# Hybrid decoder step: the output projection's weights in single blocks, a tenth expert weight buffer, token rows stored before their scaling

## What is computed

```python
# cut from the reference
proj = rmsnorm(x, norm_mix) @ w_in                # z, x/B/C, dt, u
y_ssd, y_s5 = SSD_group(proj), S5_group(proj)     # 1024 columns each, each with its own rmsnorm
x = x + concatenate([y_ssd, y_s5], -1) @ w_out    # w_out is 2048 x 1024
t = rmsnorm(x, norm_ffn)
g = argmax(t @ rc_w + rc_b)                       # one of 4 groups of experts
pick the best 2 of the group's 8 experts; gates = p_group * normalised softmax
for e in range(32):                               # w_gate, w_up 1024 x 512; w_down 512 x 1024
    out += gates[:, e:e+1] * ((silu(t @ w_gate[e]) * (t @ w_up[e])) @ w_down[e])
y = rmsnorm(x + out, norm_final)
```

## Time and profile before

| | us |
|---|---|
| median of 3 runs | 1072.44 |
| lowest and highest run | 1067.82, 1073.02 |
| the profiled execution, its own time | 1061.96 |
| its span, first to last instruction | 1059.7 |

### The profile page before, as it was taken

One profiled execution on the slowest core, in us unless ns is written; L12 is line 12 of the kernel. 1 busy time (PEld: TensorE's weight loads), 2 busy tenths in 40 slices (PEclk: granted clock), 3 DMA queues, 4 the chain that ended last, 5 costly groups with the idle time before them and its releaser, 6 DMA issues.

```text
span 1059.7 us, 17219 instructions
## 1 busy us (share of the span) xinstructions
PE 961.3 (91%) x6496; PEld 682.0 (64%) x6497; DVE 434.8 (41%) x743; ACT 331.1 (31%) x662; POOL 268.0 (25%) x510
## 2 busy tenths in 40 slices
PE   6999999999999999999999999999877788998881
PEld 5889779877776788998765555555443444554440
DVE  6999877454466898951521111111100101111112
ACT  3025323453325784322422222232212121222113
POOL 1000888888421010000012222222222112222110
PEclk9999999999999999999999999999999999999996
DMA  7585172110098744255589999999999999999994
GB/s 268 125 142 92 29 121 81 41 63 22 12 223 226 254 147 175 87 238 239 218 323 392 396 383 398 385 394 397 395 396 395 396 413 404 409 410 408 425 385 167
DMA packets 73566, 277.54 MB, mean 262 GB/s; under 512 B 36953, under 2 KB 38873, under 8 KB 56497
## 3 DMA queue, kind: packets, MB, share of 16 engines
q1 hardware_dynamic: 63020, 252.67, 65.0%
q0 software_dynamic: 8720, 19.86, 6.8%
q10 hardware_dynamic: 1780, 4.41, 1.1%
HBM read 260.17 MB, written 25.61 MB: 270 GB/s over the span
## 4 chain that ended last, share of the span: by engine, by line
PE 68%; DMA 23%; DVE 5%; issue 2%; ACT 1%; POOL 0%; SPq 0%; ACTq 0%; POOLq 0%; DVEq 0%
PE ps L653 24%; DMA sb_arena<-w_up 20%; PE ps L1023 9%; PE ps L1037 7%; PE ps L1016 7%; PE ps L919 7%; PE ps L992 2%; DMA sb_arena<-ssm_in 2%; PE ps L685 1%; PE ps L741 1%; PE ps L798 1%; DVE sb_arena L1960 1%; PE ps L772 1%; PE ps L895 1%; PE ps L1030 1%
## 5 line engine op out<-in xcount | busy, mean ns | idle before, releaser
L653 PE MATMUL ps<-sb_arena 128*128 128x264 f32 (+1 forms) x1152 | 266.9, 392 | 9.1 <-DMA sb_arena<-wi 9.1
L653 PEld LDWEIGHTS ps<-sb_arena 128*128 128x128 f32 x1152 | 218.8, 191 | 57.5 <-DMA sb_arena<-wi 9.6
L1956 DVE TENSOR_TENSOR sb_s5b<-sb_s5b,ps 128x256 f32<-128x256 f32 x36 | 22.2, 617 | 408.0 <-PE ps L1023 408.0
L1023 PE MATMUL ps<-sb_arena 128*64 128x256 f32 x1152 | 131.3, 380 | 22.0 <-DMA sb_arena<-w_up 22.0
L1037 PE MATMUL ps<-sb_arena 128*64 128x512 f32 x576 | 131.5, 598 | 20.7 <-DVE sb_arena L1960 20.7
L1016 PE MATMUL ps<-sb_arena 128*64 128x256 f32 x1152 | 132.6, 383 | 16.5 <-DMA sb_arena<-w_gate 15.8
L1016 PEld LDWEIGHTS ps<-sb_arena 128*64 128x64 f32 x1152 | 83.6, 138 | 76.3 <-DMA sb_arena<-w_gate 27.0
L1023 PEld LDWEIGHTS ps<-sb_arena 128*64 128x64 f32 x1152 | 82.5, 137 | 67.1 <-DMA sb_arena<-w_up 28.9
L1388 ACT ACTIVATE sb_kxf<-ps,sb_gate_of 64x512 f32<-64x512 f32 x36 | 24.6, 683 | 301.1 <-PE ps L1037 301.1
L1037 PEld LDWEIGHTS ps<-sb_arena 128*64 128x64 f32 x576 | 39.0, 136 | 90.1 <-issue 60.9
L1415 DVE TENSOR_TENSOR sb_arena<-sb_arena 128x64 f32<-128x64 f32 (+12 forms) x86 | 78.0, 907 | 19.5 <-DMA sb_arena<-ssm_in 12.2
...
...
## 6 DMA issues: line engine op xcount, KB each, us to landing
sb_arena<-w_gate SPq DMA_DIRECT2D x32, 2048.0 KB, 33.7
sb_arena<-w_up SPq DMA_DIRECT2D x32, 2048.0 KB, 35.9
sb_arena<-w_down SPq DMA_DIRECT2D x32, 2048.0 KB, 35.6
sb_arena<-wi SPq DMA_DIRECT2D x28, 512.0 KB, 4.0
sb_arena<-w_out SPq DMA_DIRECT2D x4, 2048.0 KB, 8.5
sb_arena<-ssm_in POOLq DMA_DIRECT2D x8, 512.0 KB, 8.9
sb_arena<-wglu SPq DMA_DIRECT2D x8, 512.0 KB, 5.0
o_ssm_s<-sb_arena POOLq DMA_DIRECT2D x8, 512.0 KB, 4.0
```

The lines of the kernel that those rows point to most:

```text
L653: last = mm(ps[:, b0 + h, 0:t1 - t0], ring[w % 3][:, k, :], src[:, k, t0:t1], start=k == 0, stop=k == KD - 1)
L1023: last = mm(ps[64 * r:64 * r + 64, 1, 0:256], xt[:, k, :], Wu[s][:, k, 256 * r:256 * r + 256], start=k == 0, stop=k == KD - 1)
L1956: V.tensor_tensor(hh.rearrange("p (j c) -> p c j", j=2), sg.rearrange("p (c j) -> p c j", j=2), ps[:, 1, 0:256].rearrange("p (c j) -> p c ...
```

## The change

`w_out` comes in sixteen loads of 512 KB, one for each block (8 x 128 columns per partition, so rows of 512 bytes), into three raw buffers; the low part of each block lies in place in them, and there are two high parts, one of them in the array kxf. A block's load waits until block o-3 is done, its high part on ACT until block o-2 is done, and PE waits before each block for its low part. The high and low parts are put one by one into the lists of ACT and DVE.

The space that this frees holds a tenth expert buffer, `Wg_first`, for the gate weights of expert 0; the three slots `Wg` then hold the gates of experts 1, 2, 3 and so on. SP's list is reordered: up 1 is loaded at the start of the projection, gate 0 when the S5 gate products are done, then up 0, gate 1, down 0 and gate 3 between the blocks' loads, down 1 when block 15 is done, then the stores into sum_scr, which no longer wait for x_scr, and then gate 2, up 2 and down 2. The refills go up, down and then the next expert's gate.

The rows are stored into x_scr as they are. ACT's five scalings are gone; the one-hot table of the first tile is multiplied with the root (oh0), and a third table, oh_root, made by DVE and ten more matmuls, gives each slot's root, which ACT applies when it copies a gathered tile. The gathered rows now lie where the rows x1 were, so POOL's first gathers wait for the stores into sum_scr as well, and the first tile's copies wait until both tables are finished (oh_done 2).

```diff
-        wo = [part(14944, KD, 512), part(4096, KD, 512)]
-        wo_hi, wo_lo, y_hi, y_lo = (
+        wo = [part(14944 + 1024 * i, KD, P) for i in range(3)]
+        wo_lo, y_hi, y_lo = (
             [rounded(f"{name}{i}", off, KD, w) for i, off in enumerate(offs)] for name, w, offs in (
-                ("wo_hi", 512, (39920, 26736)), ("wo_lo", 512, (14944, 4096)),
+                ("wo_lo", P, (14944, 15968, 16992)),
                 ("y_hi", N, (35632, 22448)), ("y_lo", N, (10656, 30832))))
...
+        Wg_first = part(4096, KD, FF)
+        xg = [part(1024 * i, D, p=(0, T)) for i in range(RING)]
         xst = part(8384, D, p=(0, T))
         xt = part(9408, KD, T)
         ht = part(9920, 2, P)
-        Lt = part(4288, N, p=(0, 36))
-        xs = [part(o, D) for o in (4824, 5848, 6872, 19040, 20064)]
-        first = part(21088, D, p=(0, T))
+        Lt = part(9806, N, p=(0, 36))
+        first = xst
+        root_of = part(10176, IDXC, p=(0, T))
...
+        kxf_at = -(-nc.sbuf_base // 32) * 32
         kxf = sb("kxf", [P, 2048 + 1024])
+        wo_hi = [rounded("wo_hi0", 18016, KD, P),
+                 nc.alloc_sbuf_tensor_at("sb_wo_hi1", [P, KD, P], F32R, offset=kxf_at)]
...
-            def wo_load(q):
-                sp.dma_start(wo[q % 2], wsrc[:, 8 * (q // 2):8 * (q // 2) + 8,
-                                             512 * (q % 2):512 * (q % 2) + 512]).then_inc(wo_ld[q % 2], 16)
+            def wo_load(o):
+                sp.dma_start(wo[o % 3], wsrc[:, 8 * (o // 8):8 * (o // 8) + 8,
+                                             P * (o % 8):P * (o % 8) + P]).then_inc(wo_ld[o % 3], 16)
             sp.wait_ge(gelu_done, 8)
-            wo_load(0)
+            for o in range(3):
+                wo_load(o)
...
+            sp.wait_ge(hn_done, NS)
+            sp.dma_start(Wu[1], usrc[1]).then_inc(wu_ld[1], 16)
+
+            def next_wo(o):
+
+                sp.wait_ge(o_mm, o - 2)
+                wo_load(o)
+
+            next_wo(3)
             sp.wait_ge(y2_done, 8)
-            sp.wait_ge(wide_done, NW)
-            wo_load(1)
-            sp.wait_ge(o_mm, 4)
-            wo_load(2)
+            sp.dma_start(Wg_first, gsrc[0]).then_inc(ld_x[0], 16)
+            for o in range(4, 7):
+                next_wo(o)
             sp.wait_ge(ms_done, 3)
             sp.dma_start(gf, a["gffn"].rearrange("(k p) -> p k", p=P), allow_slow_non_contiguous=True).then_inc(moe_ld, 16)
             sp.dma_start(g8, a["gffn"].rearrange("(p k) -> p k", k=KD)).then_inc(moe_ld, 16)
             sp.dma_start(wr, a["wr"].rearrange("p (k n) -> p k n", k=KD)).then_inc(moe_ld, 16)
             sp.dma_start(brow, a["br"].rearrange("c o -> (c o)").partition_broadcast(P)).then_inc(moe_ld, 16)
-            sp.wait_ge(o_mm, 8)
-            wo_load(3)
-            sp.dma_start(Wg[0], gsrc[0]).then_inc(wg_ld[0], 16)
-            sp.dma_start(Wg[2], gsrc[2]).then_inc(wg_ld[2], 16)
-            sp.wait_ge(o_mm, 12)
+            for o in range(7, 11):
+                next_wo(o)
             sp.dma_start(Wu[0], usrc[0]).then_inc(wu_ld[0], 16)
+            next_wo(11)
+            next_wo(12)
+            sp.dma_start(Wg[0], gsrc[1]).then_inc(wg_ld[0], 16)
+            next_wo(13)
+            next_wo(14)
             sp.dma_start(Wd_to[0], dsrc[0]).then_inc(wd_ld[0], 16)
-            sp.dma_start(Wu[2], usrc[2]).then_inc(wu_ld[2], 16)
+            next_wo(15)
+            sp.dma_start(Wg[2], gsrc[3]).then_inc(wg_ld[2], 16)
             sp.wait_ge(o_mm, 16)
-            sp.dma_start(Wg[1], gsrc[1]).then_inc(wg_ld[1], 16)
-            sp.dma_start(Wu[1], usrc[1]).then_inc(wu_ld[1], 16)
             sp.dma_start(Wd_to[1], dsrc[1]).then_inc(wd_ld[1], 16)
-            sp.wait_ge(xs_st, 80)
+            sp.wait_ge(x1t_ev, 10)
             for i, (t0, n) in enumerate(TT):
                 sp.dma_start(sum_scr[t0:t0 + n, :], x1[i][0:n]).then_inc(sum_st, 16)
-            sp.wait_ge(xtr, 2)
+            sp.dma_start(Wg[1], gsrc[2]).then_inc(wg_ld[1], 16)
+            sp.dma_start(Wu[2], usrc[2]).then_inc(wu_ld[2], 16)
+            sp.wait_ge(x1t_mm, 9)
             sp.dma_start(Wd_to[2], dsrc[2]).then_inc(wd_ld[2], 16)
             sp.wait_ge(slot_done, 1)
-            def load_expert(s, gate_src, up_src, down_src, before):
+            def load_expert(s, up_src, down_src, before):
                 done = tile_bound(sp, before, 1)
-                sp.wait_ge(gmm, done)
-                sp.dma_start(Wg[s], gate_src).then_inc(wg_ld[s], 16)
                 sp.wait_ge(umm, done)
                 sp.dma_start(Wu[s], up_src).then_inc(wu_ld[s], 16)
                 sp.wait_ge(dmm, done + 1)
                 sp.dma_start(Wd_to[s], down_src).then_inc(wd_ld[s], 16)
+            def load_gate(s, gate_src, before):
+
+                sp.wait_ge(gmm, tile_bound(sp, before, 1))
+                sp.dma_start(Wg[s], gate_src).then_inc(wg_ld[s], 16)
+
+            def of(w, e):
+                return w[bass.ds(e, 1)].rearrange("a p k n -> (a p) k n")
+
             with sp.Fori(1, E_LOOP) as ep:
                 for s in range(WBUF):
                     e = ep * WBUF + s
-                    load_expert(s, *(w[bass.ds(e, 1)].rearrange("a p k n -> (a p) k n") for w in (gsrc, usrc, dsrc)),
-                                bass.ds(e - (WBUF - 1), 1))
-            for e in range(E_LOOP * WBUF, E):
-                load_expert(e % WBUF, gsrc[e], usrc[e], dsrc[e], slice(e - WBUF + 1, e - WBUF + 2))
+                    load_expert(s, of(usrc, e), of(dsrc, e), bass.ds(e - (WBUF - 1), 1))
+                    load_gate(s, of(gsrc, e + 1), bass.ds(e - (WBUF - 2), 1))
+            load_expert(0, usrc[30], dsrc[30], slice(28, 29))
+            load_gate(0, gsrc[31], slice(29, 30))
+            load_expert(1, usrc[31], dsrc[31], slice(29, 30))
...
             pl.wait_ge(tab_ev, 1)
             pl.wait_ge(xs_st, 80)
+            pl.wait_ge(sum_st, 80)
             for u in (1, 2, 3, 0):
                 nc.gpsimd.indirect_dma_start(xg[u], None, x_scr, bass.IndirectOffsetOnAxis(ap=tok_of[:, u:u + 1], axis=0),
                                              bounds_check=N - 1, oob_is_err=False).then_inc(gath[u], 16)
-            pl.wait_ge(sum_st, 80)
...
-                q, c = o // 4, P * (o % 4)
-                yh, yl, wh, wl = y_hi[q // 2], y_lo[q // 2], wo_hi[q % 2], wo_lo[q % 2]
-                if o % 4 == 0:
-                    pe.wait_ge(wo_lod, q + 1)
+                yh, yl, wh, wl = y_hi[o // 8], y_lo[o // 8], wo_hi[o % 2], wo_lo[o % 3]
+                pe.wait_ge(wo_lod, o + 1)
                 if o >= 2:
...
+            for j in range(10):
+                last = mm(ps[0:T, 5, T:T + IDXC], oh_row[:, j, :], oh_root[:, j, :], start=j == 0, stop=j == 9)
+            last.then_inc(tab_mm, 1)
...
-            def wo_high(q):
-                ac.wait_ge(wo_ld[q % 2], 16 * (q // 2 + 1))
-                act_(wo_hi[q % 2][:], wo[q % 2], ACT.Copy).then_inc(wo_hid, 1)
+            def wo_high(o):
+                ac.wait_ge(wo_ld[o % 3], 16 * (o // 3 + 1))
+                if o >= 2:
+                    ac.wait_ge(o_mm, o - 1)
+                act_(wo_hi[o % 2][:], wo[o % 3], ACT.Copy).then_inc(wo_hid, 1)
...
+                    ac.wait_ge(ssm_out, 16)
+                    wo_high(1)
...
+            for o in range(2, 5):
+                wo_high(o)
             root_wide(1)
+            wo_high(5)
+            wo_high(6)
             for k in range(KD):
                 ac.wait_ge(y2_done, 12 + 4 * (k // 4))
                 high_part(1, sig, PF_GS5, k)
-            wo_high(2)
-            wo_high(3)
+                if k == 3:
+                    wo_high(7)
+            wo_high(8)
+            wo_high(9)
...
+                wo_high(10 + d)
                 x1_square(d)
             x1_rows(0)
             x1_rows(1)
+            wo_high(14)
             x1_square(4)
             x1_rows(2)
             x1_rows(3)
+            wo_high(15)
...
-            ac.wait_ge(xroot_done, 1)
             ac.wait_ge(x1t_ev, 10)
             for i, (t0, n) in enumerate(TT):
-                act_(xs[i][0:n], x1[i][0:n], ACT.Copy, scale=ssum[0:n, i:i + 1]).then_inc(xs_done, 1)
-                ac.wait_ge(xs_done, i + 1)
-                ac.dma_start(x_scr[t0:t0 + n, :], xs[i][0:n, :]).then_inc(xs_st, 16)
+                ac.dma_start(x_scr[t0:t0 + n, :], x1[i][0:n, :]).then_inc(xs_st, 16)
...
+            ac.wait_ge(oh_done, 2)
...
+                    act_(xst, xg[(u + 1) % RING], ACT.Copy, scale=root_of[:, bass.ds(q + 1, 1)]).then_inc(staged, 1)
...
-            def wo_low(q):
-
-                dv.wait_ge(wo_hid, q + 1)
-                V.tensor_tensor(wo_lo[q % 2][:], wo[q % 2], wo_hi[q % 2][:].bitcast(F32), ALU.subtract).then_inc(wo_lod, 1)
+            def wo_low(o):
+
+                dv.wait_ge(wo_hid, o + 1)
+                V.tensor_tensor(wo_lo[o % 3][:], wo[o % 3], wo_hi[o % 2][:].bitcast(F32), ALU.subtract).then_inc(wo_lod, 1)
             sample_update(4)
```

(20 more changed lines are left out.)

40 lines of the change are left out of this document (19 added, 21 removed).

## The result

The changed kernel is slower: **1073.97 us** in the median of 20 runs (1068.22 to 1078.26), against 1069.24 for the kernel before in the same series (20 runs, 1062.58 to 1076.53). The ratio is 1.0046, with a 95% interval of 1.0025 to 1.0067, so +4.9 us. The forecast was -2.7.

A forecast was written before the change was run, and what follows sets the result against it. The prediction took the DMA engines to bound the kernel from 545 us on and PE before that. Its terms -8.4 + 5.0 + 0.7 = -2.7 us gave 1069.7 us from a median of 1072.44, range 1062.5 to 1075.5.

The forecast's parts named there:

- The stalls: Projection, before blocks 2, 5 and 7: PE waits for DVE's low parts, +1.2, +2.6, +1.2; block 15 ends 5.0 us later.
- Rival 1: Projection: the stalls stay out through gaps in DVE's order or PE making them good; 1064.0 us, chance 0.2.
- The clock: Projection, behind the 2.6 us stall before block 5: PE's granted clock may fall; half of 1.5 counted, +0.7 us.
- rival 3: Projection: PE's clock falls after each of the three stalls, 4.1 us more; 1073.8 us, chance 0.12.
- The transfers of w_out in 512-byte rows: Projection: 512 KB loads take 4 us alone, 9 behind a 2 MB piece, and land without holding PE.
- rival 2: Projection: w_out pieces land late because 512-byte rows cost the engines 6.9 us, not 1.6; +10, 1079.6 us, chance 0.08.
- The gap between block 15 and the first refill: DMA engines were partly idle from 515 to 545 us; share forecast to rise from 0.87 to 0.95 or more.
- The step that failed: Expert stage, from 545 us: only fewer bytes left or an earlier start moves the end; DMA share 1.01 at 400 GB/s.
- the term of -8.4 us: After block 15: one 2 MB piece fewer left, 5.5 us, plus 2.9 us less DMA idling.
- The 1.2 us itself: Routing: ten matmuls of the third table lengthen it by 1.2 us, at no cost beside PE's 59 idle us.
- Idle before 3.9, now 1.0: 2.9 us: Between block 15 and the first refill: earlier stores cut DMA idle time from 3.9 to 1.0 us, gaining 2.9.
- Rival 4: Expert stage: the tenth buffer brings nothing, bound by the loop from freed buffer to refill's landing; 1075 to 1078, chance 0.1.

The follow-up runs named there:

- a_order: Changed kernel with DVE's list around the projection reordered, so low parts come ahead of the S5 root and second gate products; ratio 0.9966 to the kernel before.
- a_early: Changed kernel with shorter routing on PE: first bound read earlier, warm-up 7 steps not 9, root table's matmuls before first tile's transposes; ratio 1.0049 to the kernel before.
- b_sums: Kernel before with the sum_scr stores issued when the last rows are copied, not behind the x_scr stores; ratio 1.0023 to the kernel before.
- a_all5: a_all4 with gate 2 also loaded only after tile 1's gather has landed; 1064.18 us, ratio 0.9973 to the kernel before.
- b_late3: Kernel before with 7 extra PE matmuls (3.2 us) between the last routing table and the first expert; ratio 1.0019 to the kernel before.
- a_all3: Changed kernel with DVE's new order, shorter routing, and down 2 loaded only after tile 1's gather has landed; ratio 0.9989 to the kernel before.
- a_all4: Changed kernel with DVE's new order, shorter routing, and up 2 and down 2 loaded only after tile 1's gather has landed; 1060.06 us, ratio 0.9933 to the kernel before.
- a_two_behind: Changed kernel with up 2 and down 2 loaded behind the first tile's transposes; ratio 1.0089 to the kernel before.
- a_all2: Changed kernel with DVE's new order, shorter routing, and up 2 and down 2 behind the first tile's transposes; ratio 0.9983 to the kernel before.

## Why the prediction was wrong

The stalls were right. Before blocks 2, 5 and 7 PE waited 5.1 us in all, of which 2.6 in the longest, for the low part on DVE, in the places and for the reasons that were worked out; 5.0 was the forecast. Rival 1 (they stay out) falls with it; a_order shows that another order of the same instructions would have kept them out.

The clock was mis-sized: 0.7 was counted, 1.75 measured, all of it in block 5; the waits before blocks 2 and 7 cost none, so rival 3 was right for one stall in three. Together the projection lost 6.8 in place of 5.7.

The transfers of w_out in 512-byte rows land 3.8 us after issue in the median and no high part waits for one; rival 2 falls. The gap between block 15 and the first refill is gone (0.98), as forecast.

**The step that failed** is the first one: "from 545 us on the end moves only if fewer bytes are left when this stage starts, or if it starts earlier", with its reason, a DMA share of 1.01 over 482 us beside 59 idle us of PE. The idle time is a sum over two regimes, and the share is 1.01 in both, so it doesn't tell them apart. The windows of the kernel before, split at 745 us:

```profile
545.00:745.00 200.00, 191.73 (x1448) 1.00 1.01 390
745.00:1027.00 282.00, 231.60 (x1684) 0.99 1.01 407
```

50 of PE's 59 idle us lie behind 745. Up to there PE works through its tiles with only its short handovers between, three experts hold their buffers for a second tile, and the engines must stop when all buffers are full. In the kernel before they came to the last of these stops with 5 us in hand, so they looked like the bound; the change gave them more lead than that: one piece and the closed gap, and 3.7 us by which PE came later. Of the 8.4 us that were counted as gain, plus these 3.7, 5.1 counted: the term of -8.4 us in the sum was worth -5.1 + 3.7 = -1.4. With +5.0 + 0.7, which was measured as +6.8, that is the +5.4 of the profiles in place of -2.7.

From it follow the others:
- "The 1.2 us itself costs nothing, covered by PE's 59 idle us": it was 2.5 us, and once the 5 us of slack were used they counted in full. 1.2 of them are the ten matmuls. The other 1.3 are a later start of the one-hot product, behind a wait of 1.2 us on L1003 for which the profile names no releaser. It stands where PE reads the first bound, and in a_early, where that read comes earlier and the warm-up is shorter, it is gone. That the multiplication by the root on DVE brought it out is likely but not shown: b_sums has no such multiplication and the same wait, 1.3 us, behind a warm-up of 4.13 us in place of 5.77.
- "Idle before 3.9, now 1.0: 2.9 us": the gap was the time in which the gathers passed. Closed by itself it gained nothing (b_sums, +2.1 us in the medians) in place of 2.9.
- The gather of tile 1 wasn't in the forecast at all. Its wait of 1.1 us is the rest of the 3.7.
- Rival 4 (the tenth buffer brings nothing) named a time of 1075 to 1078, +2.6 to +5.6 us on the median that the forecast started from, and came nearest with its change. But the share is 1.00 from 545 to 745 us and 1.01 behind it, not under 0.98. Its cause is right only in part: the engines do wait for a freed buffer, but at the stops of the two-tile experts and not all through, and a piece is worth 5.7 us as soon as the engines have nothing in hand (a_all5).
- Two agreements are luck. The measured 1073.97 lies in the stated range, though the time went the other way, because the three runs of before that the forecast started from had a median of 1072.44 and the twenty of this series have 1069.24. For the same reason rival 3's 1073.8 is nearly the measured time: it stood for +1.4 us and three slow blocks, and one was slow.

The Trainium skill ("TensorE: Matmul & The Clock Gate", section "HAM oscillation — how this bites in real kernels") describes a kernel in which the engine waits for data between bursts and starts each burst at half clock. Its waits are longer than the three stalls here, so it doesn't speak for rival 3. The traces agree with it after the stall of 2.6 us before block 5. They also show that the length of the last wait doesn't decide it: in the changed kernel an up product behind a wait of 1.96 us took 5.36 us, at a granted clock of 0.70, and in b_late3 one behind 3.15 us took 3.67, at 1.00:

```profile
974.74 5.36 PE L1048 MATMUL ps<-sb_arena 128*64 128x256 f32 x32 [1.96 <-DMA sb_arena<-w_up]
```
```profile
774.84 3.67 PE L1025 MATMUL ps<-sb_arena 128*64 128x256 f32 x32 [3.15 <-DMA sb_arena<-w_up]
```

What stays open: why a gather beside running transfers takes 8.6 to 11.4 us. That it is the transfers in flight is shown by a_all3 against a_all4; how they hold it up isn't. The Trainium skill ("DMA: Bandwidth & Descriptors", section "Queues, rings and completion order") says that each DMA engine takes turns between the queues that have work, a packet at a time. The traces fit that in so far as a gather issued within 0.5 us of 4 MB (a_two_behind and a_all2, 10.7 us) fared no better than one with up 2 already running and nothing behind it (a_all3, 11.0). Two parts of the change were not tested by themselves: the new order of the refills, and the copy with a root as factor, which took 1.15 us in place of 1.06 for each gathered tile.
